# Two pads that move the operands in SBUF to multiples of 512 bytes, and another order at the head of the delta rule on VectorE

## The chip, the cores and the metric

The kernel runs on one NeuronCore of a Trainium2 chip. What counts is the time of one execution on the device, in microseconds. Three runs of the kernel before took 2759.88, 2761.99 and 2762.0 us; the median, 2761.99 us, is the time before.

## The reference

The program computes a small stack of sequence-mixing layers in float32, for 256 tokens of width 2048. It is, in this order: an even layer (one projection from 2048 to 5392 columns, sliding-window attention with 16 heads beside a gated delta rule with 8 heads, and a projection back), a gated feed-forward of width 5632, an odd layer (projection to 4096 columns, gelu, a causal mixing over chunks of 128 tokens, projection back), a second feed-forward, a final norm, and a second block with its own input projection, an attention with forget gates, a short convolution, a pooling mixer, an output projection and a layer norm.

```
h = h + even_mixer(rms_norm(h), ...)          # attention | gated delta rule
h = h + swiglu(rms_norm(h), gate, up, down)   # 2048 -> 5632 -> 2048
h = h + odd_mixer(rms_norm(h), ...)
h = h + swiglu(rms_norm(h), gate, up, down)
y = second_block(rms_norm(h), w_in_2, ..., w_out_2, ...)
```

Nearly all of the arithmetic is in the products of the 256 tokens with the weight matrices. The part that the second half of the change touches is the delta rule: for each head, and for each tile of 128 tokens, it needs a lower triangular matrix of decayed and masked products k k^T, the inverse of that matrix plus the identity, and a masked, decayed matrix of products q k^T that is multiplied with the new values at the end of the tile.

## The kernel before

**Weights as a stream.** Every product with a weight matrix is cut into blocks of 512 output columns, and each block into tiles of 128 rows by 512 columns. SyncE loads two such tiles at a time into `raw` (four slots). ScalarE casts each tile to float32r (a rounded float32), into the ring `w_hi` of 8 tiles (line 709). VectorE subtracts and puts the rest into the ring `w_lo` (line 1514). TensorE keeps the activations as the stationary operand: for each weight tile and each of the two tiles of tokens it issues three matmuls of 512 columns, high by high, high by low, low by high (lines 1023 to 1025; for the very last block lines 1007 to 1009). So each weight tile costs six matmuls and six weight loads. The activations lie as `xh` and `xl` (the 16 tiles of a normed input) or `fh` and `fl` (the 44 tiles of a feed-forward's inner width). The first block is only 272 columns wide, all others have 512.

**The last block.** Here the token tiles are run one after the other, so all sixteen weight tiles must be kept. The function `w_tile` gives the first eight of them to another pair of rings, `w2_hi` and `w2_lo`, which lie where `xh` and `xl` lay, and the others to the ordinary rings.

**Where things lie.** The tensors in a partition of SBUF follow each other in the order in which `sb(...)` and then `overlay(...)` name them. `h`, `raw`, `w_hi`, `w_lo`, `gs` and `hb` have sizes that are multiples of 4096 bytes. After them come `consts`, `cols`, `small` and `stat` (2560, 800, 672 and 1632 bytes, together 5664, which is 32 more than a multiple of 512), `extra`, `fw_hi` and `fw_lo` (multiples of 512), and then the shared region with `xh`, `xl`, `fh`, `fl`. The same region holds, at other times, the tensors of the delta rule (`dL`, `dQK`, `dD`, `dE`, `dY`, `dC`, `dkb`), of the attentions, of the odd mixer and `w2_hi` and `w2_lo`. All the sizes there are multiples of 512 bytes, so that all that starts a tile in that region has one residue.

**The mixer beside the stream.** While the weights of one block are streamed, a generator on each engine (`delta`, then `attention`) gives one step of the small work after each weight tile: `stream` calls `next(mixer)` after tile k, on VectorE four tiles later than on TensorE. A `yield` ends a step. VectorE, ScalarE and TensorE each run their instructions in program order, so what stands in a step of VectorE also delays the `w_lo` tiles after it. In `delta`, the head of a tile of tokens runs from `gam` (line 1527) to the first `dE` (line 1564), and the levels of the inversion follow. TensorE may begin level 1 (line 1076, `dL` by `dE`) when the two halves of `dE` are there and when `lqk_ready` tells that VectorE has read the products q k^T out of the banks which level 1 overwrites. Each level then makes `dY` (line 1573) on VectorE, and two matmuls (lines 1085 and 1086) that need `dY` and `dD`.

SyncE's wait before it loads into a slot of `raw` is for the `w_lo` tiles that were made from that slot (`lo_ready`), so a late VectorE also makes the next loads late.

Of the kernel before, what the change touches and what calls it, by code (L numbers as in the profile page):

```python
# [20 lines left out]
ALU = mybir.AluOpType  # L21
AX = mybir.AxisListType
# [3 lines left out]
P = 128  # L26
# [9 lines left out]
EPS = 1e-6  # L36
# [3 lines left out]
B_HEADS, B_HD = 8, 128  # L40
# [152 lines left out]
def program(nc, a, out):  # L193
# [15 lines left out]
    with ctx:  # L209
# [3 lines left out]
        def sb(name, shape, dt=F32):  # L213
            return ctx.enter_context(nc.sbuf_tensor(name, shape, dt))


        h = sb("h", [P, NT, D])
        raw = sb("raw", [P, 4, 2, BLK])
        w_hi = sb("w_hi", [P, RING, BLK], F32R)
# [7 lines left out]
        extra = sb("extra", [P, 8, SEQ])  # L227
        fw_hi = sb("fw_hi", [P, KT, 8], F32R)
        fw_lo = sb("fw_lo", [P, KT, 8], F32R)

        ident = consts[:, C_IDENT:C_IDENT + P]
        upper = consts[:, C_UPPER:C_UPPER + P]
# [9 lines left out]
        def st(*shape):  # L242
            n = int(np.prod(shape))
            v = stat[:, used[0]:used[0] + n]
            used[0] += n
            assert used[0] <= 408
            if len(shape) == 2:
                return v.rearrange("p (x y) -> p x y", x=shape[0])
            if len(shape) == 3:
                return v.rearrange("p (x y z) -> p x y z", x=shape[0], y=shape[1])  # L250
            return v
# [9 lines left out]
        o_ss, o_r, l2_q_r = st(8), st(8), st(NT, 8)  # L261
# [3 lines left out]
        def overlay(*parts):  # L265
# [15 lines left out]
        _, dL, dQK, dD, dE, _, dY, dC, dkb, masks = overlay(  # L281
            ("pad_d0", [P, 8192]), *[(n, [P, 8, P]) for n in ("dL", "dQK", "dD", "dE")],
            ("pad_d1", [P, 28 * SEQ]), *[(n, [P, 8, P]) for n in ("dY", "dC", "dkb")],
            ("level_masks", [P, LEVELS, P]))
# [15 lines left out]
        v_new = gs[:, :, :].rearrange("p t (c n) -> p (t c) n", c=4)  # L300
# [28 lines left out]
        def quarters(first, n=1):  # L329
            return ps[:, first:first + n, :].rearrange("p b (k c) -> p (b k) c", k=4)  # L330
# [22 lines left out]
        dec_in, dec_exp, kq_mm, lqk_ready, kv_ready = [sem(n) for n in (  # L353
            "dec_in", "dec_exp", "kq_mm", "lqk_ready", "kv_ready")]
        c_ready, y_mm, y_copied, de_mm, de_ready = [sem(n) for n in (
            "c_ready", "y_mm", "y_copied", "de_mm", "de_ready")]
# [3 lines left out]
        o_copied, o_sq, o_ms, o_rs, o_done = [sem(n) for n in ("o_copied", "o_sq", "o_ms", "o_rs", "o_done")]  # L360
# [817 lines left out]
        def _(dve):  # L1178
            link = linker(dve, dve_link)
            STT, TT, TS = dve.scalar_tensor_tensor, dve.tensor_tensor, dve.tensor_scalar  # L1180

            def spread(v, n, last=P):

                return v.unsqueeze(2).to_broadcast([P, n, last])

            def each(v, n):

                return v.unsqueeze(1).to_broadcast([P, n, v.shape[1]])

            def heads(v):  # L1190
                return v.rearrange("p (h c) -> p h c", h=8)
# [330 lines left out]
            def delta():  # L1522

                for t in range(NT):
# [21 lines left out]
                        four = slice(4 * half, 4 * half + 4)  # L1546
                        TT(dC[:, four, :], dL[:, four, :], each(masks[:, 0, :], 4), ALU.mult).then_inc(c_ready, 1)
                    yield
                    dve.wait_ge(c_ready, 2 * t + 2)
                    TT(dD[:, :, :], each(ident, 8), dC[:, :, :], ALU.subtract)  # L1550
                    yield
                    link(TT(dQK[:, :, :], dQK[:, :, :], each(upper, 8), ALU.mult))
                    dve.wait_ge(kq_mm, 2 * t + 2)
                    TT(dQK[:, :, :], quarters(4, 2), dQK[:, :, :], ALU.mult).then_inc(lqk_ready, 1)
                    yield
                    if t == 1:
                        dve.wait_ge(o_sq, 1)
                        link(dve.tensor_reduce(o_ss, v_new[:, :, :], AX.X, ALU.add))
                        TS(o_ss, o_ss, 1.0 / B_HD, EPS, ALU.mult, ALU.add).then_inc(o_ms, 1)
                    yield  # L1560
                    for half in range(2):
                        four = slice(4 * half, 4 * half + 4)
                        dve.wait_ge(de_mm, 2 * LEVELS * t + half + 1)
                        TT(dE[:, four, :], each(ident, 4), quarters(6 + half), ALU.subtract).then_inc(de_ready, 1)
                    yield
                    for lv in range(1, LEVELS):
                        if lv == 1:
                            dve.wait_ge(back_copied, 12)
                            TT(heads(vn[:, t, :]), heads(vn[:, t, :]), spread(beta[:, t, :], 8), ALU.mult)
                        for half in range(2):  # L1570
                            four = slice(4 * half, 4 * half + 4)
                            dve.wait_ge(y_mm, 2 * ((LEVELS - 1) * t + lv - 1) + half + 1)
                            TT(dY[:, four, :], quarters(y_bank(lv) + half), each(masks[:, lv, :], 4),
                               ALU.mult).then_inc(y_copied, 1)
                        if lv == 2:
                            scale = k_scale[:, 0, :]
                            if t == 1:
                                link(TT(k_scale[:, 1, :], beta[:, 1, :], e_gam[:, 1, :], ALU.mult))
                                scale = k_scale[:, 1, :]
                                dve.wait_ge(s_mm, 1)  # L1580
                            TT(dkb[:, :, :], heads(kn[:, t, :]), spread(scale, 8), ALU.mult).then_inc(kv_ready, 1)
                        if lv == 3 and t == 1:
                            TT(q_dec[:, :, :], q_dec[:, :, :], dqT[:, :, tok], ALU.mult).then_inc(q_scale, 1)
                        if lv < 4:
                            yield
                        for half in range(2):
                            four = slice(4 * half, 4 * half + 4)
                            dve.wait_ge(de_mm, 2 * (LEVELS * t + lv) + half + 1)
                            dve.wait_ge(de_ready, 2 * (LEVELS * t + lv - 1) + half + 1)
                            if lv < LEVELS - 1:  # L1590
                                TT(dD[:, four, :], dD[:, four, :], quarters(de_bank(lv, half)), ALU.subtract)
                            TT(dE[:, four, :], dE[:, four, :], quarters(de_bank(lv, half) + 1),
                               ALU.subtract).then_inc(de_ready, 1)
                        if lv == 4 and t == 0:
                            TT(dC[:, :, :], each(upper, 8), spread(g_log[:, 1, :], 8), ALU.mult).then_inc(ug_ready, 1)
                        if lv in (4, 5) and t == 1:
                            dve.wait_ge(evac_act, by["z"][1].n_act)
                            z = heads(zs[:, lv - 4, :])
                            TT(z, z, each(onorm, 8), ALU.mult).then_inc(z_ready, 1)
                        yield  # L1600
# [170 lines left out]
```

## Time and profile before

| what | value |
|---|---|
| median of three runs | 2761.99 us |
| profiled execution, its time | 2760.72 us |
| profiled execution, its span | 2758.9 us |
| TensorE busy with matmuls | 2719.4 us, 99% of the span |
| VectorE busy | 1550.9 us, 56% |
| ScalarE busy | 1261.1 us, 46% |
| bytes moved, mean | 477.47 MB, 173 GB/s |
| granted TensorE clock, mean | 0.996 |

The span runs from the first to the last instruction of the profiled execution. Matmuls are pipelined: the profile gives each of 512 columns some 395 ns, but one starts well before the one ahead of it ends, so the pace is read from the distance of the starts. The granted clock is the share of TensorE's full clock of 2.4 GHz that was given; 0.5 is 1.2 GHz.

### The profile page before, as it was taken

Reading aid. Unit: us, or ns where it says so; the run is one execution under the profiler, and the core shown is the slowest. Engines: PE = TensorE matmul, PEld = TensorE weight load, DVE = VectorE, ACT = ScalarE, POOL = GpSimd, SP = SyncE. Lnnn points to the kernel's source line nnn. Section 1 sums busy time; section 2 is a strip of 40 time slices with the busy share of each in tenths; the row PEclk is TensorE's granted clock in tenths of the full one; section 3 lists DMA queues with packets and bytes.
Section 4 is the critical chain, followed back from the end, with each engine's and each line's share of the span. In section 5 each row is a group of like instructions: output and inputs, shape, how many; then the busy total and the mean of one; then the engine's idle time right before and its main releaser. Section 6 shows DMA issues by size and latency. Waiting matters only on the chain.

```text
span 2758.9 us, 35364 instructions
## 1 busy us (share of the span) xinstructions
PE 2719.4 (99%) x12523; PEld 2210.9 (80%) x12523; DVE 1550.9 (56%) x2553; ACT 1261.1 (46%) x2381; POOL 28.9 (1%) x34
## 2 busy tenths in 40 slices
PE   8999999999999999999999999999999999999998
PEld 7878877888888888888788888888888887888876
DVE  6876756654545455554555555545455555565655
ACT  6452145544444444444555544444444444444433
POOL 1000000000000000000000000000000000000000
PEclk9999999999999999999999999999999999999999
DMA  7552223656565655556555656555655555555564
GB/s 222 171 167 68 70 92 110 190 182 186 182 186 181 185 183 188 185 185 221 160 172 183 193 176 192 179 188 181 189 181 186 186 187 153 168 173 166 175 228 154
DMA packets 251152, 477.47 MB, mean 173 GB/s; under 512 B 19080, under 2 KB 22912, under 8 KB 250400
## 3 DMA queue, kind: packets, MB, share of 16 engines
q1 hardware_dynamic: 245808, 467.92, 54.2%
q10 hardware_dynamic: 4656, 7.15, 0.7%
q8 instruction: 71, 1.16, 0.2%
q0 software_dynamic: 576, 0.90, 0.1%
q14 instruction: 41, 0.34, 0.0%
HBM read 473.82 MB, written 2.10 MB: 173 GB/s over the span
## 4 chain that ended last, share of the span: by engine, by line
PE 92%; DVE 5%; ACT 1%; issue 1%; DMA 1%; SPq 0%; ACTq 0%; POOL 0%; DVEq 0%
PE ps L1023 28%; PE ps L1025 28%; PE ps L1024 28%; PE ps L807 2%; DVE gs L1239 1%; DVE w_lo L1514 1%; PE ps L1086 1%; PE ps L1085 1%; PE ps L1076 1%; DMA raw<-in_even_w_in 1%; ACT w_hi L709 0%; DVE gs L1237 0%; PE ps L1165 0%; PE ps L1009 0%; PE ps L1008 0%
## 5 line engine op out<-in xcount | busy, mean ns | idle before, releaser
L1514 DVE TENSOR_TENSOR w_lo<-raw,w_hi 128x512 fp32r<-128x512 f32 (+1 forms) x1776 | 1157.0, 686 | 784.7 <-ACT w_hi L709 780.4
L709 ACT CAST w_hi<-raw 128x512 fp32r<-128x512 f32 (+1 forms) x1776 | 1030.6, 621 | 756.7 <-PE ps L1025 634.1
L1023 PE MATMUL ps<-w_hi,xh 128*128 128x512 f32 (+1 forms) x2464 | 986.7, 400 | 6.4 <-DVE w_lo L1514 5.0
L1025 PE MATMUL ps<-w_hi,xl 128*128 128x512 f32 (+1 forms) x2464 | 972.5, 395 | 0.0
L1024 PE MATMUL ps<-w_lo,xh 128*128 128x512 f32 (+1 forms) x2464 | 972.5, 395 | 0.0
L1023 PEld LDWEIGHTS ps<-w_hi,xh 128*128 128x128 f32 x2464 | 464.2, 188 | 117.9 <-DVE w_lo L1514 14.2
L1025 PEld LDWEIGHTS ps<-w_hi,xl 128*128 128x128 f32 x2464 | 463.8, 188 | 110.2
L1024 PEld LDWEIGHTS ps<-w_lo,xh 128*128 128x128 f32 x2464 | 464.3, 188 | 103.5
L1023 PE MATMUL ps<-w_hi,fh 128*128 128x512 f32 x1056 | 422.5, 400 | 5.4 <-DVE w_lo L1514 5.4
L1025 PE MATMUL ps<-w_hi,fl 128*128 128x512 f32 x1056 | 418.9, 397 | 0.0
L1024 PE MATMUL ps<-w_lo,fh 128*128 128x512 f32 x1056 | 418.9, 397 | 0.0
L1023 PEld LDWEIGHTS ps<-w_hi,fh 128*128 128x128 f32 x1056 | 199.0, 188 | 55.9 <-issue 8.8
L1025 PEld LDWEIGHTS ps<-w_hi,fl 128*128 128x128 f32 x1056 | 199.2, 189 | 48.0
L1024 PEld LDWEIGHTS ps<-w_lo,fh 128*128 128x128 f32 x1056 | 199.3, 189 | 46.4
L1301 DVE SCALAR_TENSOR_TENSOR hb<-ps,stat,gs 128x512 f32<-128x512 f32 x44 | 31.0, 747 | 97.5 <-PE ps L1025 97.5
L583 ACT CAST fh<-ps 128x512 f32 (+1 forms) x44 | 23.6, 590 | 121.0 <-PE ps L807 121.0
L578 ACT ACTIVATE gs<-ps,stat 128x512 f32<-128x512 f32 x44 | 27.8, 682 | 108.5 <-PE ps L1025 108.5
L1423 DVE TENSOR_TENSOR fl<-ps,fh 128x512 f32 (+1 forms) x52 | 33.5, 686 | 74.2 <-ACT fh L583 63.2
L1289 DVE TENSOR_TENSOR h<-ps,h 128x512 f32<-128x512 f32 x40 | 25.7, 685 | 57.7 <-PE ps L1025 57.7
L516 ACT ACTIVATE gs<-h 128x512 f32<-128x512 f32 x40 | 25.2, 631 | 67.9 <-DVE h L1289 67.4
L1201 DVE SCALAR_TENSOR_TENSOR xl<-ps,cols,xh 128x256 fp32r<-128x256 f32 x80 | 33.5, 478 | 30.8 <-ACT xh L523 30.8
L523 ACT ACTIVATE xh<-ps,cols 128x256 fp32r<-128x256 f32 x80 | 31.9, 476 | 30.1 <-PE ps L807 30.1
(292 smaller groups left out, 1108.4 us busy)
## 6 DMA issues: line engine op xcount, KB each, us to landing
raw<-in_ffn_w_gate SPq DMA_DIRECT2D x176, 512.0 KB, 4.5
raw<-in_ffn_w_up SPq DMA_DIRECT2D x176, 512.0 KB, 4.6
raw<-in_ffn_w_down SPq DMA_DIRECT2D x176, 512.0 KB, 4.3
raw<-in_w_in SPq DMA_DIRECT2D x112, 512.0 KB, 3.8
raw<-in_even_w_in SPq DMA_DIRECT2D x80, 512.0 KB, 3.7
raw<-in_odd_w_in SPq DMA_DIRECT2D x64, 512.0 KB, 4.4
raw<-in_even_w_out SPq DMA_DIRECT2D x32, 512.0 KB, 3.7
raw<-in_odd_w_out SPq DMA_DIRECT2D x32, 512.0 KB, 4.8
```

Of the source, the lines that this page charges most:

```text
L523: ins = act.activation(xh[:, kt + kk, :], halves(bank + c)[:, kk, :], ACT.Copy, scale=cols[:, gain + kt + kk:gain + kt + kk + 1])
L578: act.activation(gs[:, t, :], acc(p, t), ACT.Silu, scale=rstd[:, p.norm, t:t + 1]).then_inc(evac_act, 1)
L709: act.copy(w_tile(w_hi, w2_hi, blk, k), raw[:, slot, kk, 0:blk.width]).then_inc(hi_ready, 1)
L807: ins = pe.transpose(halves(bank + c)[:, kk, P * t:P * (t + 1)], rows(t, 2 * c + kk), ident)
L1023: pe.matmul(acc(blk, t), hi_x[:, blk.kt0 + k, tok], hi_w, start=(k == 0), stop=False)
L1024: pe.matmul(acc(blk, t), hi_x[:, blk.kt0 + k, tok], lo_w, start=False, stop=False)
L1025: ins = pe.matmul(acc(blk, t), lo_x[:, blk.kt0 + k, tok], hi_w, start=False, stop=(k == blk.nk - 1))
L1076: ins = pe.matmul(quarters(y_bank(lv) + half)[:, i, :], dL[:, hd, :], dE[:, hd, :], start=True, stop=True)
L1201: ins = STT(xl[:, kt + kk, :], halves(bank + c)[:, kk, :], cols[:, gain + kt + kk:gain + kt + kk + 1], xh[:, kt + kk, :].bitcast(F32), ALU ...
L1301: STT(hb[:, t, :], acc(p, t), rstd[:, p.norm, t:t + 1], gs[:, t, :], ALU.mult, ALU.mult).then_inc(evac_dve, 1)
L1423: TT(fl[:, kt, :], halves(4 + c), fh[:, kt, :].bitcast(F32), ALU.subtract).then_inc(pt_read, 1)
L1514: TT(w_tile(w_lo, w2_lo, blk, k), raw[:, slot, kk, 0:w], w_tile(w_hi, w2_hi, blk, k).bitcast(F32), ALU.subtract).then_inc(lo_ready, 1)
```

## The change

Two unused tensors are allocated. `pad_h` takes 96 floats (384 bytes) ahead of `h` and so moves everything behind it. `pad_x` takes 120 floats (480 bytes) behind `fw_lo` and so moves only the shared region. The pads put the rings at a multiple of 512 bytes. Counted back, `h`, `raw`, `w_hi` and `w_lo` lay 128 bytes beyond such a multiple before (512 less 384). The shared region lay 128 + 32 = 160 bytes beyond one; with both pads, 160 + 384 + 480 = 1024, it is at a multiple too. No instruction reads or writes the pads. What lies between, `gs` and `hb` to `fw_lo`, moves by 384 bytes, so that `gs`, `hb` and `consts` start at a multiple of 512 as well.

In `delta` on VectorE, for each of the two tiles of tokens: the identity minus `dC` (which gives `dD`) moves from the step after `dC` to behind the two `dE`; the product of `dQK` with the upper mask moves from the head to level 3; at the second tile of tokens the sum of squares `o_ss` and what scales it move from ahead of `dE` to level 1. The number of steps does not change.

```diff
+        sb("pad_h", [P, 96])
         h = sb("h", [P, NT, D])
...
+        sb("pad_x", [P, 120])
...
                     yield
-                    dve.wait_ge(c_ready, 2 * t + 2)
-                    TT(dD[:, :, :], each(ident, 8), dC[:, :, :], ALU.subtract)
-                    yield
-                    link(TT(dQK[:, :, :], dQK[:, :, :], each(upper, 8), ALU.mult))
                     dve.wait_ge(kq_mm, 2 * t + 2)
                     TT(dQK[:, :, :], quarters(4, 2), dQK[:, :, :], ALU.mult).then_inc(lqk_ready, 1)
                     yield
-                    if t == 1:
-                        dve.wait_ge(o_sq, 1)
-                        link(dve.tensor_reduce(o_ss, v_new[:, :, :], AX.X, ALU.add))
-                        TS(o_ss, o_ss, 1.0 / B_HD, EPS, ALU.mult, ALU.add).then_inc(o_ms, 1)
+                    yield
                     yield
                     for half in range(2):
                         four = slice(4 * half, 4 * half + 4)
                         dve.wait_ge(de_mm, 2 * LEVELS * t + half + 1)
                         TT(dE[:, four, :], each(ident, 4), quarters(6 + half), ALU.subtract).then_inc(de_ready, 1)
+                    dve.wait_ge(c_ready, 2 * t + 2)
+                    TT(dD[:, :, :], each(ident, 8), dC[:, :, :], ALU.subtract)
                     yield
                     for lv in range(1, LEVELS):
                         if lv == 1:
                             dve.wait_ge(back_copied, 12)
                             TT(heads(vn[:, t, :]), heads(vn[:, t, :]), spread(beta[:, t, :], 8), ALU.mult)
+                            if t == 1:
+                                dve.wait_ge(o_sq, 1)
+                                link(dve.tensor_reduce(o_ss, v_new[:, :, :], AX.X, ALU.add))
+                                TS(o_ss, o_ss, 1.0 / B_HD, EPS, ALU.mult, ALU.add).then_inc(o_ms, 1)
...
+                        if lv == 3:
+                            dve.wait_ge(lqk_ready, 2 * t + 2)
+                            TT(dQK[:, :, :], dQK[:, :, :], each(upper, 8), ALU.mult)
```

## Rows read from the trace of the kernel before

**Rows 1.** The page: busy time and instructions of TensorE, and the chain by engine.
```profile
PE 2719.4 (99%) x12523; PEld 2210.9 (80%) x12523; DVE 1550.9 (56%) x2553; ACT 1261.1 (46%) x2381; POOL 28.9 (1%) x34
...
PE 92%; DVE 5%; ACT 1%; issue 1%; DMA 1%; SPq 0%; ACTq 0%; POOL 0%; DVEq 0%
```

**Rows 2.** Chain in order of time: start us, length us, what.
```profile
6.89 6.41 DMA raw<-in_even_w_in
...
17.93 7.41 DMA raw<-in_even_w_in
...
973.62 0.87 PE ps L807 x8
1019.29 0.87 PE ps L807 x8
```

**Rows 3.** Timeline of TensorE, last block: start us, length us, instruction.
```profile
2726.93 0.39 PE L1007 MATMUL ps<-w_hi,fh 128*128 128x512 f32 x1
...
2731.69 0.40 PE L1007 MATMUL ps<-w_hi,fh 128*128 128x512 f32 x1
...
2736.59 0.40 PE L1007 MATMUL ps<-w_hi,fh 128*128 128x512 f32 x1
```

**Rows 4.** Timeline of TensorE, narrower matmuls: 272 columns, then 256.
```profile
18.06 0.29 PE L1023 MATMUL ps<-w_hi,xh 128*128 128x272 f32 x1
...
22.87 0.29 PE L1025 MATMUL ps<-w_hi,xl 128*128 128x272 f32 x1
...
2321.76 0.28 PE L936 MATMUL ps<-xh,fw_hi 128*8 128x256 f32 x1
...
2322.11 0.40 PE L1023 MATMUL ps<-w_hi,xh 128*128 128x512 f32 x1
```

**Rows 5.** Timeline of TensorE at half clock, and that stretch with PEclk behind POOL.
```profile
300.64 0.63 PE L1024 MATMUL ps<-w_lo,xh 128*128 128x512 f32 x1
...
302.35 0.44 PE L1025 MATMUL ps<-w_hi,xl 128*128 128x512 f32 x1
...
300.00:303.00 3.00, 3.00 (x12) 2.47 (x12) 1.83 (x4) 0.12 (x1) 0.00 (x0) 0.60 0.54 171
```

**Rows 6.** Stretches, line 1023 alone: PE, PEld busy (count), PEclk, DMA, GB/s.
```profile
50.00:205.00 155.00, 79.39 (x194) 36.62 (x195) 1.00 0.55 164
205.00:470.00 265.00, 70.42 (x162) 31.57 (x162) 0.98 0.26 82
470.00:2726.00 2256.00, 1235.05 (x3095) 581.98 (x3095) 1.00 0.59 184
```

**Rows 7.** Stretches, all engines: PE PEld DVE ACT POOL, PEclk, DMA, GB/s.
```profile
0.00:50.00 50.00, 43.86 (x242) 37.98 (x243) 30.51 (x69) 30.52 (x73) 9.33 (x21) 1.00 0.83 254
...
470.00:2748.00 2278.00, 2274.36 (x10045) 1838.33 (x10045) 1216.63 (x1950) 1055.81 (x1896) 6.86 (x6) 1.00 0.58 183
```

**Rows 8.** Timeline of all engines, head of the first tile of tokens.
```profile
217.69 1.22 DVE L1550 TENSOR_TENSOR dD<-consts_sb,dC 128x1024 f32<-128x1024 f32 x1
...
219.42 1.22 DVE L1552 TENSOR_TENSOR dQK<-dQK,consts_sb 128x1024 f32<-128x1024 f32 x1
...
219.80 0.63 ACT L709 CAST w_hi<-raw 128x512 fp32r<-128x512 f32 x1 [0.72 <-PE ps L1025]
...
221.82 1.28 DVE L1514 TENSOR_TENSOR w_lo<-raw,w_hi 128x512 fp32r<-128x512 f32 x2
223.02 1.28 DVE L1564 TENSOR_TENSOR dE<-consts_sb,ps 128x512 f32<-128x512 f32 x2
...
223.75 2.05 PE L1076 MATMUL ps<-dE,dL 128*128 128x128 f32 x16 [1.72 <-DVE dE L1564]
...
227.03 0.38 PE L1085 MATMUL ps<-dD,dY 128*128 128x128 f32 x2
```

**Rows 9.** Timeline of all engines, head of the second tile of tokens.
```profile
293.93 1.14 ACT L709 CAST w_hi<-raw 128x512 fp32r<-128x512 f32 x2 [3.13 <-DMA raw<-in_even_w_in]
...
295.09 1.21 DVE L1558 TENSOR_REDUCE stat<-gs 128x8 f32<-128x1024 f32 x1
...
297.01 1.28 DVE L1564 TENSOR_TENSOR dE<-consts_sb,ps 128x512 f32<-128x512 f32 x2
297.75 2.67 PE L1076 MATMUL ps<-dE,dL 128*128 128x128 f32 x16 [3.94 <-DVE dE L1564]
...
302.62 0.38 PE L1085 MATMUL ps<-dD,dY 128*128 128x128 f32 x2
```

## The prediction

> **What bounds the kernel now.** I read the busy time and the chain of the page first. TensorE is busy for 2719.4 of 2758.9 us, and 92% of the chain is its own [rows 1]. The stretches say where that holds: from 470 us to the end of the stream TensorE is busy for 2274.36 of 2278 us, while VectorE works for 1216.63, ScalarE for 1055.81 and the DMA engines for a 0.58 share [rows 7]. Nobody makes TensorE wait there, so only fewer or faster matmuls can shorten it. Before 470 us it is otherwise: in the first 50 us the DMA share is 0.83 [rows 7] and two pieces of the chain, 6.41 and 7.41 us, are loads [rows 2]; at the heads of the delta rule TensorE stands idle for VectorE, 1.72 us once and 3.94 us once [rows 8, 9].
>
> So I read the pace of the matmuls next. One gate and one up block lie between two sets of transposes: 45.67 us less 0.87 us of transposes, for 2 x 16 x 6 = 192 matmuls, is 233.3 ns each [rows 2]. 512 columns at 2.4 GHz are 213.3 ns. So 20 ns of every matmul are not columns. Half clock shows what kind of loss this is: at 1.2 GHz four matmuls take 1.71 us, 427.5 ns each, and 512 columns are 426.7 ns [rows 5]. The loss is all but gone when TensorE asks for its data at half the rate. So it is no fixed price of an instruction; it looks like the supply of the operands from SBUF.
>
> The last block then shows that this supply depends on where the operand lies. Its first eight weight tiles lie in the shared region, at residue 160 (bytes beyond a multiple of 512), its other eight in the ordinary rings, at residue 128; the stationary operands `fh` and `fl` are the same kind in both, at residue 160. From 2726.93 to 2731.69 us 21 matmuls start, 226.7 ns each; from 2731.69 to 2736.59 us again 21, 233.3 ns each [rows 3]. The same engine, clock, shape and line, and 6.6 ns apart. The address counts.
>
> **The pads.** What does residue 0 for both operands give? No row shows it, so I bound it. Narrower matmuls split the loss into a part per column and a part per matmul. At residue 128 the first block's 272 columns take (22.87 - 18.06) / 38 = 126.6 ns [rows 4]; against 233.3 ns for 512 that is 106.7 / 240 = 0.445 ns a column, and 5.7 ns are left. At residue 160, three matmuls of 256 columns take 0.35 us, 116.7 ns each [rows 4]; against 226.7 ns that is 0.430 ns a column, and 6.7 ns are left. A column at 2.4 GHz is 0.4167 ns. So the part per column differs with the residue (0.028 and 0.013 ns over the clock), as if each crossing of a 512-byte line cost something, and the part per matmul hardly does. A tile of 2048 bytes crosses four such lines from residue 128 or 160, and three from 0, and none of its pieces is then short. If the part per column goes and the part per matmul stays, the pace is 213.3 + 6.7 = 220.0 ns. If all goes but what half clock leaves (0.8 ns), it is 214.1 ns. In the other direction the nearest rows are 226.7 ns (what a ring at the residue of its stationary operand has), 233.3 ns (no effect), and one step of 6.7 ns the other way, 240.0 ns. I take the middle of the two good ends, 217.0 ns, because each fact in the rows ties the loss to the place of the moving tile within 512 bytes, and a start at 0 is the one place where no piece is short.
>
> The count: line 1023 runs 3095 times from 470 us on [rows 6], lines 1024 and 1025 as often, and the last block has 16 x 2 x 3 = 96, together 9381 matmuls. At 233.3 - 217.0 = 16.3 ns that is 152.9 us. Between 50 and 470 us there are 3 x (194 + 162) = 1068 more [rows 6]. There TensorE waits for VectorE now and then, and a faster TensorE will wait longer; of 17.4 us I take half, 8.7 us (ends: nothing and all of it). In the first 50 us I take nothing, since loads end the waits there. What comes next: VectorE's 1216.63 us and ScalarE's 1055.81 us stay far below the 2120 us or so that this stretch will then have, and the DMA share goes from 0.58 to about 0.62, below the 0.83 that the first 50 us reach [rows 7]. No other engine becomes the bound.
>
> A rule of the Trainium skill speaks against the pads. "SBUF — State Buffer", in its section on the DMA port swizzle, says that SBUF has lines of 16 bytes and that an access is at full rate when consecutive reads fall in the same line. Residues 0, 128 and 160 are all multiples of 16, so by this rule the pads would change nothing and the time would be that of the rival "no effect" below; the two paces of the last block [rows 3] disagree with it. For the good case only a page has a price: "TensorE: Matmul & The Clock Gate", in its section on why the gap is 56 ns and not 53.3, gives N / 2.4 + about 2.5 ns between starts of bf16 matmuls, which is an estimate of 215.8 ns here and would make the time about 2587 us; no row here shows it.
>
> **The loads.** `raw` and its rows of 2048 bytes move to residue 0 too. Over most of the span a faster load shortens nothing, as the DMA engines have room. In the first 50 us it could: the two pieces of the chain are 13.8 us [rows 2] and bound the gain; no row shows that a load's time depends on its address, and I take 0. VectorE and ScalarE also get other addresses; I take 0, hidden under TensorE from 470 us on.
>
> **The head of the first tile of tokens.** Two of VectorE's instructions of 1.22 us leave the way to `dE`, that for `dD` and the mask of `dQK` [rows 8]. What ends last then? VectorE has a `w_lo` tile to make from the cast that ends at 220.43 us, and makes it until about 221.1 us. So `dE` is written from 221.1 to 222.4 us, not from 223.02 us on. TensorE, which has issued its last stream matmul by then, begins at about 222.0 instead of 223.75 us: 1.7 us less. But `dD` now stands between `dE` and `dY`: 222.4 + 1.22 (`dD`) + 0.6 (`w_lo`) + 1.22 (scaling of v) + 0.65 (the first half of `dY`) = 226.1 us. TensorE would be free for line 1085 at about 222.0 + 1.8 + 1.4 = 225.2 us and waits until 226.1 us; it got there at 227.03 us before [rows 8]. So 0.9 us of the 1.7 are kept. New waits: `dE` stands in front of VectorE's queue until the transposes of `dC` are done, and behind it are the `w_lo` tiles; here they are done before.
>
> **The head of the second tile.** Here the cast of a pair of weight tiles waits for its load until 293.93 us [rows 9]. The load is tied to `w_lo` tiles that were made before any moved instruction, so it doesn't come earlier. VectorE makes the pair from 294.5 to 295.7 us and then `dE`, 1.3 us earlier than 297.01 us. Behind it come `dD`, `w_lo`, the scaling of v, and now also the reduction and its scaling, 1.21 + 0.17 us: 297.0 + 1.22 + 0.6 + 1.22 + 1.4 + 0.65 = 302.1 us for the first half of `dY`, and line 1085 started at 302.62 us before [rows 9]. So 0.5 us are kept, and the idle time ahead of line 1076 is still 2.6 us, so I leave the half clock behind it as it is. The mask of `dQK` in level 3, 1.22 us for each tile of tokens, is read only behind the last level; I cost it at nothing, because after `dY` TensorE has matmuls of its own, and at 1.22 us each if that cover is gone. Sum of the reordering: 1.4 us less. Its ends: 6.9 us less, if both waits (1.72 and 3.94 us) go and with them the half clock, of which the rows show six matmuls at 194 ns too much; 3.8 us more, if the moved 2 x 1.22 and 1.4 us are all uncovered.
>
> **The sum.** 152.9 + 8.7 + 1.4 = 163.0 us. The profiled execution took 2760.72 us (its span 2758.9), 1.3 us under the median of 2761.99 us, so I take the sum from the median: 2599 us. At 220.0 ns it is 124.8 + 7.1 + 1.4 = 133.3 us, so 2629 us; at 214.1 ns 180.1 + 10.3 + 1.4 = 191.8 us, so 2570 us.
>
> **The rivals.**
> *Only the distance counts.* In the last block's first half both operands have the same residue, and there the pace is 226.7 ns; it may be their distance within 512 bytes that matters and not their place. Then the pads bring all matmuls to 226.7 ns: 61.9 + 3.5 + 1.4 = 66.8 us less, 2695 us. For it: the rows can't tell distance from place. Against it: the matmuls of 256 columns load only 8 columns as stationary operand and still lose 10 ns each [rows 4], so a clash with weight loads isn't the whole of it.
> *No effect.* The cost may follow the place within 64 or 128 bytes, where 0 and 128 are alike; or the faster rings may be faster because they lie in another region of SBUF. Then only the reordering stays, 2760.6 us. For it: residue 160 is the less round number and the faster one. Against it: nothing in the rows but the part per column.
> *The operands collide.* This is the one on the other side. A weight load of 128 columns runs beside every matmul. If loads and moving tiles that start at the same place in a line want the same part of SBUF at once, each matmul loses a step of 6.7 ns more, 240.0 ns: 9381 and 1068 matmuls give 62.9 + 7.2 us more, less 1.4 us, 2831 us. It decides as soon as a pace over 233.5 ns shows. Against it: equal residues are the faster case in [rows 3].
>
> **How the numbers follow.** Forecast (214 to 220 ns) 0.50, distance 0.18, no effect 0.20, collision 0.12. This kernel's runs tell a difference of about 0.2%, 5.5 us, from none. The first two are faster, 0.68; "no effect" is 1.4 us, with ends of 6.9 us less and 3.8 us more, so of its 0.20 I give 0.06 to faster, 0.13 to the same and 0.01 to slower. Faster 0.74, same 0.13, slower 0.13. The range goes from the good end, 2570 us, to 2762 us, so that the distance and nearly all of "no effect" are in; what is left out is the collision and a little below 2570 us. The forecast's own range is 2570 to 2629 us.
>
> **What would show it.** In the profile after, a gate and up pair between transposes should take about 42.5 us instead of 45.67 us, in all of its blocks, and the two halves of the last block should have one pace. 44.4 us there would be the distance, 45.7 us no effect. At half clock the pace should stay at 427.5 ns. `dE` should follow `w_lo` at once, TensorE's wait for it should be near 0 at the first tile and 2.6 us at the second, and line 1085 should wait for `dY` at both. The prediction is wrong if the pace stays over 224 ns, or if the pace falls and TensorE then waits for casts or loads in the feed-forwards.

## The result, and the profile after

The kernel after takes 2693.51 us (median of four runs, 2692.71 to 2695.8), the kernel before 2760.93 us in the same comparison: a ratio of 0.9758, 95% interval 0.9741 to 0.9775. The forecast was 2599 us. The kernel is faster, as forecast, but the gain is 67.4 us where 163 us were forecast; the time is within 2 us of the rival "only the distance counts" (2695 us). Part of that nearness is luck, as the account of the gain below shows.

The page after, busy time and the chain by engine, as in [rows 1]:

```profile
PE 2652.1 (99%) x12523; PEld 2204.8 (82%) x12523; DVE 1547.9 (58%) x2553; ACT 1262.5 (47%) x2381; POOL 28.6 (1%) x34
...
PE 91%; DVE 6%; ACT 1%; issue 1%; DMA 0%; ACTq 0%; SPq 0%; POOL 0%; DVEq 0%
```

TensorE still bounds the kernel; it is busy for 67.3 us less, with the same 12523 matmuls. VectorE and ScalarE do the same work in the same time. Then the chain in order of time, two sets of transposes around one gate and one up block, against [rows 2]:

```profile
951.32 0.87 PE ps L810 x8
995.76 0.88 PE ps L810 x8
```

44.44 us instead of 45.67: less 0.87, for 192 matmuls, that is 226.9 ns each instead of 233.3. And TensorE's timeline of the last block, against [rows 3], its first eight weight tiles and then its other seven:

```profile
2659.24 0.39 PE L1010 MATMUL ps<-w_hi,fh 128*128 128x512 f32 x1
...
2664.00 0.39 PE L1010 MATMUL ps<-w_hi,fh 128*128 128x512 f32 x1
...
2668.76 0.39 PE L1010 MATMUL ps<-w_hi,fh 128*128 128x512 f32 x1
```

21 matmuls take 4.76 us in both halves, 226.7 ns. Before, the second half had 233.3. All of the kernel now has the pace that eight weight tiles had before. The stretches, line 1026 (the counterpart of 1023) alone and then all engines, against [rows 6, 7]:

```profile
470.00:2659.00 2189.00, 1210.37 (x3082) 578.65 (x3082) 1.00 0.60 189
```

```profile
470.00:2680.00 2210.00, 2206.11 (x10007) 1827.47 (x10006) 1210.95 (x1946) 1053.83 (x1889) 6.87 (x6) 1.00 0.59 188
```

From 470 us on TensorE is busy for 2206.11 of 2210 us, so nobody makes it wait. Where the gain lies can be read from when the same instruction starts in both profiled executions. The kernel after is 0.6 us ahead at 206 us, 7.0 us when the attention's first transposes start (377.5 us before, 370.5 after), 8.7 us at 467.03 us (458.34 after), 67.7 us when the last block starts (2726.25 against 2658.56) and 68.0 us at the last matmul.

Not all of this is the change. The granted clock was at its lower level, 1.2 GHz (0.50), in four stretches of 3.4 us of the profiled execution before, and in none of the one after until its end. Four stretches before, then all of the stream after; PEclk stands behind POOL:

```profile
299.00:302.40 3.40, 3.40 (x14) 2.92 (x13) 2.83 (x4) 0.00 (x0) 0.00 (x0) 0.50 0.49 154
363.90:367.20 3.30, 3.30 (x10) 2.53 (x9) 0.67 (x2) 0.00 (x0) 0.00 (x0) 0.50 0.69 227
462.90:466.20 3.30, 3.30 (x9) 2.57 (x8) 3.30 (x7) 1.94 (x4) 0.00 (x0) 0.50 0.63 207
2654.30:2657.60 3.30, 3.30 (x9) 2.59 (x8) 1.29 (x2) 1.86 (x4) 0.00 (x0) 0.50 1.00 410
```

```profile
13.00:2685.00 2672.00, 2644.88 (x12493) 2198.05 (x12491) 1540.36 (x2537) 1256.05 (x2366) 28.22 (x29) 1.00 0.56 177
```

At the second of them the lead of the kernel after grows from 5.3 to 6.9 us, at the third from 7.1 to 8.7 us: each such stretch costs about 1.6 us, all four 6.3 us. They are not a mark of either kernel. A second profiled execution of the kernel after (after_again below) has two of them,

```profile
359.20:362.60 3.40, 3.40 (x9) 2.64 (x9) 0.86 (x2) 0.00 (x0) 0.00 (x0) 0.50 0.64 206
458.20:461.60 3.40, 3.40 (x9) 2.65 (x8) 3.40 (x7) 1.98 (x5) 0.00 (x0) 0.50 0.69 235
```

and took 2696.81 us where the first took 2692.71 us (0.9 us of the difference is there at 206 us already). So the 68.0 us between the two profiled executions are 57.8 us of faster matmuls from 467 us on (68.0 less 8.7, less 1.6 for the fourth stretch), some 3.0 us of shorter waits at the heads of the delta rule (see the order alone), 6.3 us of clock, and 0.9 us for all the rest.

The head of the second tile of tokens, all engines, against [rows 9]:

```profile
291.11 1.28 DVE L1560 TENSOR_TENSOR dE<-consts_sb,ps 128x512 f32<-128x512 f32 x2
291.64 1.14 ACT L712 CAST w_hi<-raw 128x512 fp32r<-128x512 f32 x2 [3.08 <-DMA raw<-in_even_w_in]
...
291.84 2.05 PE L1079 MATMUL ps<-dE,dL 128*128 128x128 f32 x16 [0.37 <-DVE dE L1560]
...
294.89 0.40 PE L1028 MATMUL ps<-w_hi,xl 128*128 128x512 f32 x1
...
295.18 1.21 DVE L1570 TENSOR_REDUCE stat<-gs 128x8 f32<-128x1024 f32 x1
...
297.24 0.49 PE L1088 MATMUL ps<-dD,dY 128*128 128x128 f32 x2 [1.95 <-DVE dY L1575]
```

The wait for `dE` is 0.37 us instead of 3.94, and `dE` is begun before the cast of the pair that was loaded late, not after it. In its place stands a wait of 1.95 us for `dY`, behind `dD`, the scaling of v and the reduction that was moved there. The stretch in which the clock fell before [rows 5] has all of it now (PEclk is the column after POOL):

```profile
300.00:303.00 3.00, 3.00 (x23) 2.74 (x22) 2.50 (x6) 0.50 (x1) 0.00 (x0) 1.00 0.00 0
```

At the first tile of tokens TensorE no longer waits for `dE`, and waits for `dY` instead, against [rows 8]:

```profile
220.07 1.28 DVE L1560 TENSOR_TENSOR dE<-consts_sb,ps 128x512 f32<-128x512 f32 x2
...
224.88 0.49 PE L1088 MATMUL ps<-dD,dY 128*128 128x128 f32 x2 [0.35 <-DVE dY L1575]
```

### The profile page after: what moved, and what is told of

Same layout as the page of the kernel before. It is cut to its first block, busy times and chain, and to the rows that moved or that the text cites. A ratio compares the mean times of both kernels' runs of the same rounds, so it can differ in the third digit from the quotient of the medians.

```text
span 2690.8 us, 35362 instructions
## 1 busy us (share of the span) xinstructions
PE 2652.1 (99%) x12523; PEld 2204.8 (82%) x12523; DVE 1547.9 (58%) x2553; ACT 1262.5 (47%) x2381; POOL 28.6 (1%) x34
## 4 chain that ended last, share of the span: by engine, by line
PE 91%; DVE 6%; ACT 1%; issue 1%; DMA 0%; ACTq 0%; SPq 0%; POOL 0%; DVEq 0%
PE ps L1026 28%; PE ps L1028 28%; PE ps L1027 28%; PE ps L810 2%; DVE gs L1242 1%; DVE w_lo L1517 1%; PE ps L1089 1%; PE ps L1088 1%; ACT w_hi L712 0%; PE ps L1079 0%; DVE gs L1240 0%; PE ps L1168 0%; PE ps L1012 0%; PE ps L1010 0%; PE ps L1011 0%
## 5 line engine op out<-in xcount | busy, mean ns | idle before, releaser
L1026 PE MATMUL ps<-w_hi,xh 128*128 128x512 f32 (+1 forms) x2464 | 971.9, 394 | 7.7 <-DVE w_lo L1517 7.0
L1028 PE MATMUL ps<-w_hi,xl 128*128 128x512 f32 (+1 forms) x2464 | 957.8, 389 | 0.0
L1027 PE MATMUL ps<-w_lo,xh 128*128 128x512 f32 (+1 forms) x2464 | 956.6, 388 | 0.0
L1026 PE MATMUL ps<-w_hi,fh 128*128 128x512 f32 x1056 | 414.8, 393 | 5.6 <-DVE w_lo L1517 5.6
L1028 PE MATMUL ps<-w_hi,fl 128*128 128x512 f32 x1056 | 411.3, 390 | 0.0
L1027 PE MATMUL ps<-w_lo,fh 128*128 128x512 f32 x1056 | 411.0, 389 | 0.0
```

The source lines that it names most:

```text
L1026: pe.matmul(acc(blk, t), hi_x[:, blk.kt0 + k, tok], hi_w, start=(k == 0), stop=False)
L1027: pe.matmul(acc(blk, t), hi_x[:, blk.kt0 + k, tok], lo_w, start=False, stop=False)
L1028: ins = pe.matmul(acc(blk, t), lo_x[:, blk.kt0 + k, tok], hi_w, start=False, stop=(k == blk.nk - 1))
```

## The experiments

Two theories stood against each other: D, the distance of the moving and the stationary operand within 512 bytes sets the pace; P, the place of the moving tile does. The kernel after cannot tell them apart, as it has distance 0 and residue 0 at once.

**The second pad alone.** Distance 0 at residue 128, the slow one of [rows 3].

```diff
         fw_lo = sb("fw_lo", [P, KT, 8], F32R)
+        sb("pad_x", [P, 120])
```

> The kernel before with the second pad alone (480 bytes behind fw_lo) and the old order on VectorE: rings at residue 128 as before, the shared region at 640, so also at 128. Distance 0 at a place that was slow. Theory D (distance): 226.7 ns a matmul in all blocks, 2761 - 65 = 2696 us. Theory P (place of the moving tile): 233.3 ns, 2761 us, and in the last block both halves alike at 233.3 ns.

Measured: 2699.8 us, ratio 0.9782 (0.9767 to 0.9797). The chain of this kernel, around a gate and up pair:

```profile
956.49 0.87 PE ps L809 x8
1000.91 0.87 PE ps L809 x8
```

44.42 us, 226.8 ns a matmul, with the rings where they were. Theory P is wrong, and so is the rival that the faster rings are faster for the region they lie in: a pad of 480 bytes behind the rings brings nearly the whole gain.

**The first pad alone.** Rings at residue 0, distance 32 as before.

```diff
+        sb("pad_h", [P, 96])
         h = sb("h", [P, NT, D])
```

> The kernel before with the first pad alone (384 bytes ahead of h) and the old order: rings at residue 0, the shared region at 160 + 384 = 544, so at 32. Distance 32 bytes, as in the kernel before, at a new place. Theory D: 233.3 ns, 2761 us. Theory P: 226.7 ns, 2696 us. The last block's first half has moving and stationary operand both at 32: theory D says 226.7 ns there.

Measured: 2759.24 us, ratio 0.9997 (0.9988 to 1.0007), no difference. The chain:

```profile
974.95 0.87 PE ps L808 x8
1020.63 0.87 PE ps L808 x8
```

45.68 us, 233.4 ns. To put the rings at a multiple of 512 bytes is worth nothing by itself.

**Every pair of residues.** A kernel without the reference's work, that only runs matmuls; each group is a line of its own:

```
for o_, s_, m_ in trio(32, 40): ins = pe.matmul(o_, s_, m_, start=True, stop=True)
# trio(m, s): (SH, MH), (SH, ML), (SL, MH) in turn, S[:, s:s+128] by M[:, m:m+512]; m, s in floats
```

> This kernel leaves the reference's work out: it copies x to the output, and beside that runs only float32r matmuls, 128 stationary columns by 512 moving ones, a weight load each. 144 groups of 12 matmuls, one line each, for every pair of 12 residues of the moving tile and 12 of the stationary one (0, 32, 64, 96, 128, 160, 192, 224, 256, 320, 384, 448 bytes beyond a multiple of 512). Read is the pace of each line. Theory D (only the distance of the two within 512 bytes counts): 226.7 ns on the diagonal, equal residues, whatever the residue, and 233.3 ns for a stationary operand 32 bytes further on than the moving one. Theory P (the place of the moving tile counts): one pace for each residue of the moving tile, whatever the stationary one's: 226.7 ns for 0 and 160, 233.3 ns for 128. Theory S (the place of the stationary operand counts too): no line of the table is constant. If any pair is near 216 ns, there is room left that the pads did not take.

Pace in ns, from the distance of the first and the last start of a group (5 of the 12 residues):

```
moving \ stationary     0      32     128     160     256
  0                   226.7  232.8   231.7   233.5   226.7
 32                   232.1  226.7   233.5   231.7   233.5
128                   231.7  233.5   226.6   232.9   231.7
160                   234.3  232.9   233.5   226.6   233.5
256                   229.0  232.9   231.7   233.5   226.6
```

The diagonal is fast at all twelve residues (226.6 to 228.6 ns), so theory D holds; a period of 256 bytes shows in the corner (0, 256). Its counterpart (256, 0), the first group behind a change of the moving residue, is in between at 229.0 ns. Nothing in any of the 144 groups is under 226.6 ns, so the 217.0 ns of the forecast are not there at any residue.

**A second pad of 736 bytes,** rings at 0 and the shared region at 256.

```diff
-        sb("pad_x", [P, 120])
+        sb("pad_x", [P, 184])
```

> The kernel after with a second pad of 184 floats instead of 120: rings at residue 0, the shared region at 256. Theory D with a period of 512 bytes: over 229 ns a matmul, over 2715 us. Theory D with the period of 256 bytes that map1 shows (226.7 ns for moving 0 and stationary 256): 226.7 ns and 2693.5 us, as the kernel after.

Measured: 2694.88 us, ratio 0.9764 (0.9749 to 0.9779), as the kernel after. In its chain a pair takes 44.44 us:

```profile
952.51 0.87 PE ps L810 x8
996.95 0.87 PE ps L810 x8
```

So the period is 256 bytes and not 512.

**Other types, other widths.** Again a kernel of matmuls alone.

> Like map1, the reference's work is left out, x is copied to the output, and matmuls run alone. Groups of 12, one line each, moving tile at residue 0: (a) distances of 0, 4, 8, 16, 24, 28, 32, 48, 112, 144, 208, 224, 240, 248, 252, 512, 1024, 2048 and 2112 bytes; (b) 8 to 128 stationary columns at distances 0, 32, 64, 192; (c) 64 to 480 moving columns at the same four; (d) plain float32, bfloat16 and float32r of 512 columns at the same four. Theory D, with the period of 256 bytes that map1 shows: 226.7 ns at 0, 512, 1024, 2048, and a higher pace elsewhere. If it is a clash of the weight load with the moving stream, the difference of distances 0 and 32 (6.2 ns at 128 columns) shrinks with fewer stationary columns and is near 0 at 8, and what is left over the column time at distance 0 shrinks too. If it belongs to the moving stream alone, the number of stationary columns changes nothing. Float32 and bfloat16, which ask for fewer bytes per ns, should show next to none of it, 2 x 430 ns a float32 matmul and about 216 ns a bfloat16 one.

The bfloat16 groups at distances 0 and 64, timeline of TensorE:

```profile
248.82 2.75 PE L154 MATMUL ps<-MB,SB 128*128 128x512 bf16 x12
...
254.00 2.75 PE L156 MATMUL ps<-MB,SB 128*128 128x512 bf16 x12
```

The next lines start at 251.41 and 256.59 us, so 12 matmuls take 2.59 us, 215.8 ns, at both distances, and at the other two as well. Plain float32 takes 429.2 ns for each of its two passes at all four. So among these three types the dependence on the distance, and the loss beyond 2.5 ns, belong to float32r alone, the one that takes 4 bytes a partition for each column at the full rate. For bfloat16 that is 2.5 ns over the column time. By "TensorE: Matmul & The Clock Gate" of the Trainium skill, in its section on the gap of 56 ns, it should be about 2.5; the trace agrees for bfloat16, and float32r in this kernel does not reach it.

Of the other distances, in groups of 12 float32r matmuls: 228.5 ns at 512 bytes and 226.6 ns at 1024 and 2048; 230 to 233 ns from 4 to 28 bytes; 226.6 ns at 252 bytes, but 233.3 at 248. With fewer stationary columns (512 moving ones, again groups of 12, ns):

```
stationary columns \ distance     0      32      64     192
  8                             230.7   229.0   231.6   231.7
 16                             231.7   231.7   231.7   231.7
 32                             231.7   236.2   231.6   231.7
 64                             228.9   231.4   233.0   232.2
 96                             229.9   228.9   228.9   233.7
128                             227.5   232.9   233.5   229.8
```

Only with 128 stationary columns is distance 0 clearly the fast one here. A stretch at half clock lay over nearly all of the groups with 128 and part of those with 256 moving columns (from 156 to 170 us); these are not used.

**Longer groups.** 36 matmuls each.

> The reference's work is left out again, x is copied to the output. Groups of 36 matmuls, moving tile at residue 0: 32 distances of the stationary operand in steps of 16 bytes; 8 and 64 stationary columns at distances 0, 32, 64, 128, 192; 256 to 496 moving columns at 0 and 32. Theory D with a period of 256 bytes: the curve from 0 to 240 and that from 256 to 496 are the same, each with one low point, 226.7 ns, at its start. If it is a clash of the weight load with the moving stream, 8 stationary columns are faster than 226.7 ns; map2 showed 231.7 ns at every distance, which speaks against it, and this group of 36 is long enough to tell an effect of the start from a pace. If the loss is per matmul, 256 columns lose about as much as 512 at the same distance; if per column, half.

The first matmul of each of four neighbouring groups, distances 256, 272, 288 and 304 bytes, and then of three with 8 stationary columns, distances 0, 32 and 64:

```profile
182.85 0.39 PE L86 MATMUL ps<-MH,SH 128*128 128x512 f32 x1
...
191.01 0.39 PE L87 MATMUL ps<-MH,SH 128*128 128x512 f32 x1
...
199.18 0.39 PE L88 MATMUL ps<-MH,SH 128*128 128x512 f32 x1
...
207.57 0.40 PE L89 MATMUL ps<-MH,SH 128*128 128x512 f32 x1
...
316.22 0.39 PE L102 MATMUL ps<-MH,SH 128*8 128x512 f32 x1
...
324.38 0.40 PE L103 MATMUL ps<-MH,SH 128*8 128x512 f32 x1
...
332.70 0.40 PE L104 MATMUL ps<-MH,SH 128*8 128x512 f32 x1
```

36 matmuls take 8.16 and 8.17 us (226.7 and 226.9 ns) at 256 and 272 bytes, and 8.39 us (233.1 ns) at 288. All 32 distances, in ns:

```
distance      0     16    32    48    64    80    96    112   128   144   160   176   192   208   224   240
from 0      226.7 226.7 233.2 233.3 233.2 231.8 234.3 233.4 233.5 233.4 233.3 229.9 228.9 233.3 233.4 227.2
from 256    226.7 226.7 233.2 233.3 233.2 231.9 234.3 233.4 233.5 233.4 233.3 229.9 228.9 233.3 233.4 227.2
```

The curve repeats after 256 bytes, with a low place from 240 to 272 and a lesser one at 176 to 192; only one low place had been expected. With 8 stationary columns distance 0 is fast too (8.16 us, 226.7 ns) and 32 is not (8.32 us, 231.1 ns). The weight load has 16 times fewer columns there (88 ns a load in the trace, 188 with 128 columns) and the difference goes from 6.4 to 4.4 ns only: it does not follow the length of the load. With 64 stationary columns distance 0 is not the fastest: 230.0 ns there, 231.6 at 32, 232.7 at 64, 229.5 at 128 and 228.3 at 192. A state also plays in: at 16 bytes a group of 12 was at 233.3 ns in the run ahead of this one, and one of 36 at 226.7 here; and distance 0 once more, as the last group of this run, was at 227.9 ns. "TensorE: Matmul & The Clock Gate" of the Trainium skill, in its step by step of a matmul, says that two independent read ports let the load of the next weights run without taking from the running matmul. The bfloat16 groups give no sign against it; the float32r groups do, since the place of the one operand against the other changes the pace by 6 ns. What the two operands share is not shown.

Narrower moving tiles at distance 0, as loss over 0.4167 ns a column: 13.1 ns at 256 columns, 13.4 at 320, 14.1 at 384, 16.3 at 448, 17.0 at 480, 13.3 at 496 and at 512. It is a loss per matmul and hardly one per column, and at distance 32 (11.6 ns at 256, 13.3 at 320, 384 and 480, 17.7 at 448, 20.0 at 496 and 19.9 at 512) it jumps rather than grows. So at 256, 384 and 480 columns distance 32 is the faster one, by 0.8 to 3.7 ns, and map2, behind its stretch at half clock, has 256 columns at 113.4 and 113.3 ns with distances 64 and 192, a loss of 6.7 ns. What the pads give this kernel holds for 512 moving columns.

**The order alone.** The kernel after without its pads.

```diff
-        sb("pad_h", [P, 96])
...
-        sb("pad_x", [P, 120])
```

> The kernel after without both pads: only the new order at the head of each tile. The working of the prediction: 1.4 us less than the kernel before, ends 6.9 us less and 3.8 us more. The rival, that the moved instructions are uncovered later, says 1 to 4 us more. In its trace TensorE's wait for dE should be near 0 us at the first tile and 2.6 us at the second, and line 1085's counterpart should wait for dY.

Measured: 2755.95 us against 2759.82, ratio 0.9983 (0.9974 to 0.9992), so 2 to 7 us less. The head of its second tile, all engines:

```profile
291.50 1.28 DVE L1558 TENSOR_TENSOR dE<-consts_sb,ps 128x512 f32<-128x512 f32 x2
292.02 1.14 ACT L710 CAST w_hi<-raw 128x512 fp32r<-128x512 f32 x2 [3.02 <-PE ps L1026]
...
292.24 2.05 PE L1077 MATMUL ps<-dE,dL 128*128 128x128 f32 x16 [0.22 <-DVE dE L1558]
...
297.63 0.49 PE L1086 MATMUL ps<-dD,dY 128*128 128x128 f32 x2 [1.95 <-DVE dY L1573]
```

The wait for `dE` is 0.22 us, not the expected 2.6; that for `dY` is there. Against the execution before, this one is 0.3 us ahead at 206 us and 4.9 us at 341 us, behind both heads; 1.6 us of that is the stretch at half clock that it doesn't have at 299 us. So the order itself is worth some 3.0 us, twice what I worked out. The rest of its 7.8 us at the last matmul is clock: two more stretches before are missing here, and one, from 2645 us, takes the place of the fourth.

**Both pads, the old order** (pads_only), and **both at residue 128, the new order** (both_128, the kernel after without its first pad; this is its edit).

```diff
-        sb("pad_h", [P, 96])
```

> The kernel before with both pads and the old order on VectorE. If pads and order add up: the change's 67.4 us less the 3.9 us of the order alone, 63.5 us, so 2697 us. The working of the prediction with the pace of 226.7 ns says 61.9 + 3.5 = 65.4 us, 2695 us. If the order is worth more with faster matmuls, since VectorE is late more often, the time is over 2698 us.

Measured: 2699.59 us, ratio 0.9777 (0.9764 to 0.9791).

> The kernel after without the first pad: both operands at residue 128, and raw, w_hi, w_lo, h at 128 as in the kernel before. Theory D alone: no difference from the kernel after, 2693.5 us. If a multiple of 512 has a worth of its own (the loads into raw, or casts on ScalarE and VectorE), 1 to 4 us more than the kernel after, as pad_x_only's 2699.8 us against 2696 expected hints.

Measured: 2696.34 us, ratio 0.9769 (0.9755 to 0.9782). The intervals of this kernel and of the kernel after (0.9741 to 0.9775) overlap, so residue 0 has no worth of its own that these runs could tell from nothing.

**The side work behind `dY`, with the kernel after beside it.**

```diff
                         if lv == 1:
-                            dve.wait_ge(back_copied, 12)
-                            TT(heads(vn[:, t, :]), heads(vn[:, t, :]), spread(beta[:, t, :], 8), ALU.mult)
...
                             TT(dY[:, four, :], quarters(y_bank(lv) + half), each(masks[:, lv, :], 4),
                                ALU.mult).then_inc(y_copied, 1)
+                        if lv == 1:
+                            dve.wait_ge(back_copied, 12)
+                            TT(heads(vn[:, t, :]), heads(vn[:, t, :]), spread(beta[:, t, :], 8), ALU.mult)
...
```

> The kernel after with the scaling of v and the reduction to o_ss behind the two halves of dY in level 1 instead of ahead of them. In the trace after, line 1088 starts 0.75 us behind the last stream matmul at the first tile and 2.35 us at the second, and 0.23 us is the pace; both waits are for dY. If the 1.22 us and 1.38 us ahead of dY are what fills them, they go: 0.5 + 2.1 = 2.6 us less than the kernel after. If TensorE then waits for something else (dD, or w_lo behind the moved work), 0 to 1 us less.

> The kernel after, unchanged, beside side_after_dY on the same chip, so that these two can be compared: 0.976 of the kernel before, as measured first. Its distance from pads_only (2699.6 us) and order_only (2756.0 us) also tells whether pads and order add up: 60.9 + 4.6 = 65.5 us if they do.

Measured: 2689.72 us (2689.23 to 2693.31), ratio 0.9748 (0.9735 to 0.9762); the kernel after beside it 2693.01 us (2692.51 to 2696.81), ratio 0.9757 (0.9743 to 0.9770). The medians are 3.3 us apart, against 2.6 expected, and the intervals overlap. The trace is clear on the place. Waits from 205 to 345 us (engine and line, for whom: us in total, times, longest), the kernel after and then this one:

```profile
PE ps L1088 <- DVE dY L1575: 3.4, 4, 2.0
```

```profile
PE ps L1088 <- DVE dY L1568: 1.1, 2, 0.5
```

2.3 us of TensorE's waits are gone, both heads' among them. This version has the lowest median of all; that it beats the kernel after is likely, not shown at 95% by the times. The profiled execution of this version and the first one of the kernel after are both at full clock up to their ends and can be laid side by side: this one is 0.5 us ahead at 206 us, before anything moved, and 3.5 us at the last matmul, so the move gave some 2.9 us. Pads and order add up within what can be told: 60.9 us (pads alone) and 3.9 (order alone) by the medians, 64.8, against 67.5 in this comparison, with an uncertainty of some 3 us on each.

## Why the prediction was wrong

*Bound, right.* TensorE's own pace set the end before and sets it after; from 470 us on no other engine and no load became late (busy for 2206.11 of 2210 us).

*That the address counts, right;* it was read from two paces in the last block, and every kernel of matmuls shows it.

*The pace at residue 0, wrong, and this is the step that failed.* In the prediction it reads "each fact in the rows ties the loss to the place of the moving tile within 512 bytes", and from it "the part per column goes": 217.0 ns. Measured are 226.7. The rows of the last block had two readings, place and distance, since the stationary operand stood at residue 160 in both halves; I noted the second as a rival and gave it 0.18. pad_x_only and pad_h_only decide it. What drew me to place was the split of the loss into a part per column and a part per matmul. That split put a line through two points each, and the points were of different kinds: the 256 columns came from matmuls with 8 stationary columns, whose `fw_hi` slices lie at changing distances. map3 shows that the loss is no line at all: 13.1 ns at 256 columns and 13.3 at 512 with distance 0. The stream from 467 us on gave 57.8 us by its pace, where 152.9 us were forecast: over 9381 matmuls that is 6.2 ns each. So the term was mis-sized by its price, 16.3 against 6.2 ns, and hardly by its count (the 48 matmuls of the last block's first half were at 226.7 ns already and gained nothing).

*The argument against distance, no argument.* I held against it that matmuls with 8 stationary columns still lose 10 ns each, so that a clash with weight loads isn't the whole of it. That much is right: the 13.3 ns that are left at distance 0 do not go away with a short load. But it says nothing on what distance changes: map3 has 226.7 and 231.1 ns with 8 columns too.

*The order, right in kind and too small.* The waits for `dY` came where they were forecast, 0.35 and 1.95 us. At the second tile I took the pair that was cast at 293.93 us [rows 9] for the pair that VectorE makes ahead of `dE`. It was not: VectorE was four tiles behind, and what it made at 294.49 us came from an earlier burst of casts. With two instructions of 1.22 us fewer ahead of them these tiles come earlier, and `dE` comes before that pair's cast. So the wait of 3.94 us went to 0.22 us and not to 2.6, and the order is worth 3.0 us instead of 1.4.

*The clock, left as it was.* I kept the half clock at 300 us and did not look for others; the profiled execution before had four stretches of it, 6.3 us in all. The first of them follows the wait of 3.94 us. All four profiled kernels with the old order have it, and of the six profiled executions with the new order one does: apart_256 waits 0.36 us for `dE` and 1.95 us for `dY`, as the kernel after does, and still has

```profile
295.60:298.90 3.30, 3.30 (x17) 3.30 (x17) 0.88 (x3) 0.00 (x0) 0.67 (x1) 0.50 0.00 0
```

So the shorter wait makes this fall rarer as far as ten profiled executions tell, and does not rule it out; that it is the cause is not shown. What sets the other stretches stays open.

*From 50 to 470 us, too much for the pads.* I took half of what 1068 faster matmuls could give. With both pads and the old order (pads_only), whose profiled execution has the same stretches at half clock there as the one before, the lead grows from 2.54 us at 206 us to 2.95 us at 467 us, so 0.4 us of the 3.2 us that 486 matmuls could give at 6.6 ns. TensorE's waits listed for that stretch are 0.6 us longer than before; where the rest went is not shown. The 7.0 us of the kernel after at 377 us are the order's 3.0 and two stretches of clock, 3.1, before anything else.

*The nearness to 2695 us, in part luck.* That sum is 61.9 + 3.5 + 1.4 us. In the profiled executions the terms are 57.8, less than 3.5 and 3.0 us, and 6.3 us of clock fill what is missing.

*The loads, right:* an aligned `raw` shows no effect, both_128 against the kernel after.

## What to carry to other kernels

Where one kind of matmul sets the time, compute its pace from the distance of starts and ask what is over the column time; if two buffers show two paces, vary each operand's address by itself before believing in a round number. Here a pad between the operands was the cure, and the pad ahead of both did nothing: 128 by 512 float32r operands want the same address modulo 256 bytes; for narrower ones these runs give no such rule. Before a difference of a few us is put down to a change, count the stretches at half clock in both traces. When instructions are taken from ahead of a wait, follow which tile an instruction really makes, as a queue that is several tiles behind is not limited by the cast beside it.

## What was not expected of the hardware

Float32r matmuls of 128 by 512 with a weight load each start every 226.7 ns when moving and stationary operand are at the same address modulo 256 bytes (226.7 to 227.2 ns within 16 bytes either way in groups of 36), and every 229 to 234 ns elsewhere; bfloat16 takes 215.8 ns and a pass of plain float32 429.2 ns at every distance tried, and at half clock float32r itself takes 427.5 ns, 0.8 over its columns [rows 5]. Float32r with 64 moving columns took 111.6 ns a matmul at full clock (three groups of 12 in map2), four times its columns, with 128 moving columns 111 to 118 ns (three distances of starts, before the clock fell), and with 256 from 113.3 to 119.8 ns. Of two executions of the kernel after, one ran at full clock up to its end and the other had two stretches of 3.4 us at 0.50, about 1.6 us each. What the remaining 13.3 ns are, and why they neither grow with the columns nor shrink with the weight load, stays open; so does the state that lets a pace carry over into the groups behind it.
